# Moving the first eight dense products of a two-block decoder kernel into its key search

## The reference, cut to what matters

```python
q = (ht @ wq).reshape(t, 8, 2, 128)
sa, sb = scores of q[:, :, 0] and q[:, :, 1] against 128 keys each
va, ia = lax.top_k(sa, 16);  vb, ib = lax.top_k(sb, 16)
cand = va[..., :, None] + vb[..., None, :]          # 256 pairs for each of 8 heads
top, pos = lax.top_k(cand, 16)                      # 16 experts for each head
g = softmax(top)
a = gelu(einsum('thkd,td->thk', u_tab[eidx], ht))
out = einsum('thk,thkd->td', g * a, v_tab[eidx])
x = x + g2 * out
```

## Time and profile before

| | before |
|---|---|
| median of three runs (lowest, highest) | 2922.46 us (2916.36, 2926.57) |
| profiled execution, own time | 2922.81 us |
| its span | 2921.1 us |
| TensorE / VectorE / ScalarE / GpSimd busy, of the span | 87% / 52% / 29% / 26% |
| mean granted TensorE clock | 0.924 |
| bytes moved by DMA | 716.90 MB |

### The profile page before, as it was taken

The page is one execution under the profiler, slowest core; times in us unless marked ns, Lnnn a source line. Parts: engine busy times, 40 slices in busy tenths (PEclk is TensorE's granted clock), DMA queues, the critical chain, the costliest instruction groups (busy, mean ns, idle before and its releaser), DMA issues.

```text
span 2921.1 us, 35637 instructions
## 1 busy us (share of the span) xinstructions
PE 2540.6 (87%) x14451; PEld 1944.1 (67%) x14451; DVE 1505.6 (52%) x3249; ACT 837.0 (29%) x1443; POOL 773.5 (26%) x743
## 2 busy tenths in 40 slices
PE   5997998889688787779987947699999999999998
PEld 5684544457444444447764526699999998998887
DVE  3125565644200000025542899879988787864443
ACT  2114322133100000023431117634433343333332
POOL 0002310000100000010000019845565655524442
PEclk8997898999799899979988978899999999999999
DMA  8224400014599999962104002799999999979995
GB/s 324 106 90 177 170 29 29 29 61 173 233 421 423 420 423 421 422 259 87 58 29 158 1 0 84 235 385 393 342 378 377 375 373 349 381 297 367 367 362 210
DMA packets 191624, 716.90 MB, mean 245 GB/s; under 512 B 33176, under 2 KB 69056, under 8 KB 161888
## 3 DMA queue, kind: packets, MB, share of 16 engines
q1 hardware_dynamic: 128480, 488.06, 42.9%
q0 software_dynamic: 62976, 226.52, 20.4%
HBM read 658.02 MB, written 56.11 MB: 244 GB/s over the span
## 4 chain that ended last, share of the span: by engine, by line
PE 67%; DVE 13%; DMA 12%; ACT 3%; issue 2%; POOL 1%; SPq 0%; POOLq 0%; DVEq 0%; ACTq 0%
PE psum L3191 14%; PE psum L3178 12%; DMA arena<-w 8%; PE psum L1588 5%; PE psum L426 4%; PE psum L2608 4%; PE psum L2108 4%; PE psum L3140 3%; PE psum L929 3%; PE psum L1595 2%; PE psum L1201 2%; PE psum L1216 1%; PE psum L2259 1%; DMA arena<-v_rows,arena 1%; DVE arena L819 1%
## 5 line engine op out<-in xcount | busy, mean ns | idle before, releaser
L3191 PEld LDWEIGHTS psum<-rounded,rounded 128*128 128x128 f32 x3072 | 452.9, 188 | 28.1 <-issue 21.8
L3178 PEld LDWEIGHTS psum<-rounded,rounded 128*128 128x128 f32 x3072 | 453.5, 189 | 22.0 <-ACT rounded L3245 14.2
L3191 PE MATMUL psum<-rounded,rounded 128*128 128x320 f32 x3072 | 462.1, 311 | 5.9 <-DVE rounded L3262 5.9
L3178 PE MATMUL psum<-rounded,rounded 128*128 128x320 f32 x3072 | 461.8, 311 | 3.4 <-DVE rounded L3262 3.4
L3127 POOL DMA_INDIRECT arena<-u_rows,arena x192 | 282.2, 1470 | 255.0 <-DVE arena L3295 163.7
L3217 ACT ACTIVATE rounded<-arena 128x1024 fp32r<-128x1024 f32 x256 | 265.5, 1050 | 258.5 <-PE psum L3191 218.8
L1588 PE MATMUL psum<-arena 128*64 128x256 f32 x2048 | 262.4, 421 | 79.9 <-issue 60.6
L3262 DVE TENSOR_TENSOR rounded<-arena,rounded 128x1024 fp32r<-128x1024 f32 x256 | 312.1, 1220 | 25.2 <-ACT rounded L3217 25.2
L1588 PEld LDWEIGHTS psum<-arena 128*64 128x64 f32 x2048 | 183.4, 153 | 171.0 <-issue 124.3
L3127 POOL DMA_INDIRECT arena<-v_rows,arena x192 | 220.1, 1146 | 240.2 <-PE psum L3140 158.1
L1700 DVE COPY arena<-psum 128x256 f32<-128x256 f32 x32 | 13.6, 424 | 444.1 <-PE psum L1641 444.1
(11 more groups left out here) (441 smaller groups left out, 3341.4 us busy)
## 6 DMA issues: line engine op xcount, KB each, us to landing
arena<-w SPq DMA_DIRECT2D x96, 2048.0 KB, 27.4
arena<-uT SPq DMA_DIRECT2D x64, 1024.0 KB, 8.3
arena<-v SPq DMA_DIRECT2D x64, 1024.0 KB, 7.4
arena<-wada SPq DMA_DIRECT2D x12, 2048.0 KB, 8.8
arena<-wp SPq DMA_DIRECT2D x10, 2048.0 KB, 9.9
arena<-gd SPq DMA_DIRECT2D x64, 320.0 KB, 9.8
gd<-arena SPq DMA_DIRECT2D x8, 2048.0 KB, 17.1
xb<-arena SPq DMA_DIRECT2D x1, 12032.0 KB, 42.1
```

Of the source, the lines that this page charges most:

```text
L3178: ins = pe.matmul(PS[:, b, 0:DT], w[:, x, k, :], hv[:, y, :], k == 0 and i == 0, k == 7 and i == 2)
L3191: ins = pe.matmul(PS[:, b, 0:DT], w[:, y, x, :], gg[:, z, :], x == 0 and i == 0, x == 7 and i == 2)
```

## The change

It takes the eight u products of group 0 out of the dense stage and makes them between keys and gather. During the keys stage ScalarE copies the hidden rows and the raw weights of these eight units into rounded upper parts, and GpSimd subtracts to get the lower parts. SP loads the raw weights one unit (512 KB) at a time into space that the key weights have left. TensorE makes the eight products behind its last scores and ahead of `turn(0)`; ScalarE copies them out of PSUM (two before `exps(0)`, six after it) and SP writes them to a DRAM array `es`. Near the end of the gather stage SP reads them back (1.25 MB), and reads the first 256 columns of g for them (1 MB in four pieces); the last 64 columns are taken straight from tile 2 in SBUF. At the start of the dense stage ScalarE and VectorE do gelu, weighting and splitting of the eight before they go into their loops. The list `UNITS` is eight shorter (248), and the dots and rounds are spread again: few dots over 49 units, not 51, the other 128 over 121 units, not 125, the first 16 rounds every 7 units. On SP's queue, `g_piece(4)` and raw piece 3 now stand behind `write(2, 0)` and behind waits for VectorE's second weighted product and for that write's landing; X stays where it was, behind raw piece 5 and the last write.

```diff
+    Y = Stage(counter, "first products", "pe ac po")
+    FH = [alias(O_TEMP + 9216 + 4 * DT * i, 4 * DT) for i in range(4)]
+    o = O_TEMP + 9216 + 16 * DT
+    FU = [o, 0, 2048, 2 * RING, 2 * RING + 2048, 3 * RING, 3 * RING + 2048, RING]
+    assert o + 2048 <= 2 * O_TEMP
+    FUH = [alias(x, 1024) for x in FU]
+    FUL = [alias(x + 1024, 1024) for x in FU]
+    FP = [at(RING + 2048 + DT * i, DT) for i in range(6)] + [at(DT * i, DT) for i in range(2)]
...
+    FIRST_IN = ((0,), (1, 2), (3, 4), (5, 6), (7,))
+    FIRST_SPLIT = {4: 0, 6: 1, 7: 2, 10: 3, 11: 4, 13: 5, 14: 6}
...
+        for x, those in enumerate(FIRST_IN):
+            if x:
+                sp.wait_ge(*K.pe["q", x - 1, 3])
+            for u in those:
+                sp.dma_start(out=at(FU[u] + 1024, 1024), in_=A["uT"][u // 2, :, 1024 * (u % 2):1024 * (u % 2) + 1024]).then_inc(
+                    *d_fu[x]("unit", u))
         wait_all(sp, K)
         sp.wait_ge(*d_xs["hs"])
+        sp.wait_ge(*Y.ac["out", 5])
+        sp.dma_start(out=es[:, 0:6 * DT], in_=at(RING + 2048, 6 * DT)).then_inc(*d_es())
+        sp.wait_ge(*Y.ac["out", 7])
+        sp.dma_start(out=es[:, 6 * DT:8 * DT], in_=at(0, 2 * DT)).then_inc(*d_es())
...
+        for u in range(8):
+            pe.wait_ge(*Y.po["lower", u])
+            if u > 2:
+                pe.wait_ge(*Y.ac["out", u - 3])
+            else:
+                pe.wait_ge(*K.ac["q", 3, u])
+            w = [x[u][:, :].rearrange("p (k b) -> p k b", k=8) for x in (FUH, FUL)]
+            for k in range(8):
+                hv = first_rows(k // 2)[:, :, k % 2, :]
+                for i, (x, y) in enumerate(THREE):
+                    ins = pe.matmul(PS[:, u % 3, 0:DT], w[x][:, k, :], hv[:, y, :], k == 0 and i == 0, k == 7 and i == 2)
+            ins.then_inc(*Y.pe("product", u))
...
+        def first_split(u):
+            ac.wait_ge(*first_there(u))
+            ac.activation(FUH[u][:, :], at(FU[u] + 1024, 1024), ACT.Copy).then_inc(*Y.ac("upper", u))
...
+            ac.activation(first_rows(y)[:, 0], H2[:, 2 * y:2 * y + 2, 0:DT], ACT.Copy).then_inc(*Y.ac("rows", y))
...
+            if c in FIRST_SPLIT:
+                first_split(FIRST_SPLIT[c])
         scores(15)
+        first_split(7)
         wait_all(ac, K)
...
+            po.wait_ge(*Y.ac["rows", y])
+            v = first_rows(y)
+            po.tensor_tensor(v[:, 1], H2[:, 2 * y:2 * y + 2, 0:DT], v[:, 0].bitcast(F32), ALU.subtract).then_inc(*Y.po("rows", y))
+        for u in range(8):
+            po.wait_ge(*Y.ac["upper", u])
+            po.tensor_tensor(FUL[u][:, :], at(FU[u] + 1024, 1024), FUH[u][:, :].bitcast(F32), ALU.subtract).then_inc(
+                *Y.po("lower", u))
...
+        pe.wait_ge(*Y.ac["out", 7])
...
+            ac.wait_ge(*Y.pe["product", u])
+            ac.activation(FP[u], PS[:, u % 3, 0:DT], ACT.Copy).then_inc(*Y.ac("out", u))
+
+        product(0)
+        product(1)
         exps(0)
+        for u in range(2, 8):
+            product(u)
...
-    UNITS = [("u", 0, a) for a in range(8)]
+    UNITS = []
...
-        DOTS.setdefault(4 + 4 * k // 5 if k < FEW else 56 + 125 * (k - FEW) // 128, []).append(k)
-    WEIGHTS = {56: 0, 182: 1}
-    ROUND = {62 + 15 * r // 2: r for r in range(FEW_ROUNDS)}
-    ROUND.update({190 + 2 * r: FEW_ROUNDS + r for r in range(32)})
-    FOLD = {181: 0, 255: 1}
+        DOTS.setdefault(3 + 49 * k // 64 if k < FEW else 52 + 121 * (k - FEW) // 128, []).append(k)
+    WEIGHTS = {52: 0, 174: 1}
+    ROUND = {58 + 7 * r: r for r in range(FEW_ROUNDS)}
+    ROUND.update({182 + 2 * r: FEW_ROUNDS + r for r in range(32)})
+    FOLD = {173: 0, len(UNITS) - 1: 1}
...
+        sp.wait_ge(*d_gd[1][3]["g", 1])
+        sp.wait_ge(*d_es.end())
+        sp.dma_start(out=at(FB, 8 * DT), in_=es).then_inc(*d_first())
+        sp.wait_ge(*d_gd[1][0]["g", 1])
+        sp.wait_ge(*G.dv["h", 3])
+
+        for p in range(4):
+            sp.dma_start(out=at3(GSL[p], 2, DT)[:, :, 0:256], in_=gd[:, 2 * p:2 * p + 2, 0:256]).then_inc(*ring[3 + p]("g", p))
         wait_all(sp, G)
+        write(2, 0)
         sp.wait_ge(*d_small.end())
         sp.dma_start(out=H2S, in_=hs[:, :, DT:512]).then_inc(*d_hrest("rest"))
-        sp.dma_start(out=gd[:, 0:8, 256:DT], in_=g_of(2)[:, 0:8, :]).then_inc(*d_first())
-        write(2, 0)
...
+        sp.wait_ge(*E.dv["weighted", 0, 1])
+        sp.wait_ge(*d_gd[0][0]["g", 2])
+        g_piece(sp, 4)
         piece(3)
-        sp.wait_ge(*E.ac["split", 2])
-        sp.wait_ge(*d_first.end())
-        for p in range(4):
-            g_piece(sp, p)
         write(2, 1)
...
+        def product(a):
+            ac.activation(at(FB + DT * a, DT), at(FB + DT * a, DT), ACT.Gelu_apprx_tanh).then_inc(*E.ac("gelu", 0, a))
+
+        split(0)
+        split(1)
+        ac.wait_ge(*d_first.end())
+        product(0)
+        product(1)
+        split(2)
+        for a in range(8):
+            ac.wait_ge(*E.dv["weighted", 0, a])
+            if a == 3:
+                ac.wait_ge(*d_gd[0][0]["g", 2])
+            if a in (5, 6):
+                ac.wait_ge(*E.dv["gg", 0, 2 * a - 9])
+            ac.activation(gg_of(0, a)[:, 0, :], at(FB + DT * a, DT), ACT.Copy).then_inc(*E.ac("gg", 0, a))
+            if a < 6:
+                product(a + 2)
...
+        def product(a):
+
+            e, p = at(FB + DT * a, DT), a // 2
+            dv.wait_ge(*E.ac["gelu", 0, a])
+            dv.tensor_tensor(e[:, 256:DT], e[:, 256:DT], g_of(2)[:, a, :], ALU.mult).then_inc(*E.dv())
+            dv.wait_ge(*ring[3 + p]["g", p])
+            dv.tensor_tensor(e[:, 0:256], e[:, 0:256], at(GSL[p] + DT * (a % 2), 256), ALU.mult).then_inc(*E.dv("weighted", 0, a))
+
         wait_all(dv, G)
-        for j in range(AHEAD):
-            split(j)
-        dv.wait_ge(*d_hrest["rest"])
-        dv.tensor_copy(H2T.rearrange("p (k c t) -> p k c t", k=8, c=2),
-                       H2S[:, :, 0:FEW].unsqueeze(2).to_broadcast([128, 8, 2, FEW])).then_inc(*E.dv("twice"))
+        split(0)
+        split(1)
+        product(0)
+        product(1)
+        split(2)
+        for a in range(8):
+            gg = gg_of(0, a)
+            dv.wait_ge(*E.ac["gg", 0, a])
+            dv.tensor_tensor(gg[:, 1, :], at(FB + DT * a, DT), gg[:, 0, :].bitcast(F32), ALU.subtract).then_inc(*E.dv("gg", 0, a))
+            if a < 6:
+                product(a + 2)
+            if a == 3:
+                dv.wait_ge(*d_hrest["rest"])
+                dv.tensor_copy(H2T.rearrange("p (k c t) -> p k c t", k=8, c=2),
+                               H2S[:, :, 0:FEW].unsqueeze(2).to_broadcast([128, 8, 2, FEW])).then_inc(*E.dv("twice"))
```

More of the change, by code:

```diff
@@ L2560, in build, with first_rows, first_there @@
     WQ = (0, 2, 3, 1)
+    Y = Stage(counter, "first products", "pe ac po")
[6 more added lines that the diff above has]
+    FP = [at(RING + 2048 + DT * i, DT) for i in range(6)] + [at(DT * i, DT) for i in range(2)]
+    es = nc.dram_tensor("es", [128, 8 * DT], F32, kind="Internal").ap()
+    FIRST_IN = ((0,), (1, 2), (3, 4), (5, 6), (7,))
+    FIRST_SPLIT = {4: 0, 6: 1, 7: 2, 10: 3, 11: 4, 13: 5, 14: 6}
+    d_fu = [dma_counter(f"first{i}") for i in range(5)]
+    d_es = dma_counter("products")
+    def first_rows(y):
+        return FH[y][:, :].rearrange("p (s k t) -> p s k t", s=2, k=2)
+    def first_there(u):
+        x = (u + 1) // 2
+        return d_fu[x]["unit", FIRST_IN[x][-1]]
     def norm3_sums(pe, i):
@@ L2627, in keys_ac @@
             ac.activation(H2[:, k, :], H2[:, k, :], ACT.Identity, bias=MOD[:, 24 + k:25 + k]).then_inc(*N3.ac("shift", k))
+        ac.wait_ge(*N3.ac["shift", 7])
+        for y in range(4):
+            ac.activation(first_rows(y)[:, 0], H2[:, 2 * y:2 * y + 2, 0:DT], ACT.Copy).then_inc(*Y.ac("rows", y))
         for c in range(16):
@@ L2728, in build @@
     assert o <= O_IT
-    GGR = [alias(x, 2 * DT) for x in early + late]
+    FB = late[3]
+    assert late[6] == FB + 6 * DT
+    GGR = [alias(x, 2 * DT) for x in early + late[1:3] + late[3:5] + late[0:1] + late[5:7]]
     o = OW
@@ L2820, in one_hots, with product @@
                 *G.ac("hot", q4))
+        def product(u):
+            ac.wait_ge(*Y.pe["product", u])
+            ac.activation(FP[u], PS[:, u % 3, 0:DT], ACT.Copy).then_inc(*Y.ac("out", u))
+        product(0)
+        product(1)
         exps(0)
+        for u in range(2, 8):
+            product(u)
         for q4 in range(LEAD):
@@ L2829, in gather_ac @@
                     one_hots(q4 + LEAD)
+                if x4 == 0 and m == 1:
+                    ac.wait_ge(*d_es.end())
                 if x4 == 0 and m > 1:
@@ L3015, in build @@
     for k in range(ALL_DOTS):
-        DOTS.setdefault(4 + 4 * k // 5 if k < FEW else 56 + 125 * (k - FEW) // 128, []).append(k)
-    WEIGHTS = {56: 0, 182: 1}
-    ROUND = {62 + 15 * r // 2: r for r in range(FEW_ROUNDS)}
-    ROUND.update({190 + 2 * r: FEW_ROUNDS + r for r in range(32)})
-    FOLD = {181: 0, 255: 1}
```

(16 more changed lines are left out.)

2 lines of the change are left out of this document (removed).

## The result

In 20 timed runs of each, the kernel after took 2927.9 us as its median (2917.62 to 2935.54), the kernel before 2920.1 (2907.98 to 2928.82). The ratio is 1.0027, 95% interval 1.0015 to 1.004: slower by 7.8 us. The forecast was 2920, a little faster than before, in a range of 2902 to 2933. The time lies in that range, but the change is a small loss, not a small gain.

A forecast was written before the change was run, and what follows sets the result against it. It took TensorE and equally full DMA engines to bound the dense stage, and VectorE's search the keys stage's end. Terms -7.4 + 0.6 + 0 + 4.3 gave -2.5 on 2922.81: 2920.3, so 2920 us, range 2902 to 2933.

The forecast's parts named there:

- Removed, 28.16 us: Dense stage: eight u units of 24 matmuls go, 3.52 us each at the full clock, 28.16 us in all.
- the first reading: Dense stage: DMA engines as full as TensorE, so removed TensorE work frees time only where bytes come as much sooner.
- The products' new place, +0.6: Between keys and gather: three products at once, 9.6 us idle, five ending about 1.0 us after VectorE's pairs; cost +0.6 us.
- Rival C: Keys stage: GpSimd's subtractions hold up VectorE's search, up to 10 us beyond its slack, 2930 us; chance 0.05.
- The mutual exclusion: Keys search: GpSimd and two-input VectorE instructions shut each other out; seven pair sums, up to 17 us, within VectorE's slack.
- The start, -7.4: Start of dense stage: fourth v unit waits for X, landing about 1940.3, and ends at 1947.1, not 1954.55; 7.4 us gained.
- the forecast's own lower end: Start of dense stage: gathers take more of the DMA engines, X comes at 1946, and the gain is 1.7 us.
- Rival D: Start of dense stage: X lands at 1946 or later, TensorE isn't brought forward, 2926 us; chance 0.08.
- The rest of the dense stage, +4.3: First 16 rounds: all become short, so TensorE's waits for v rows go from 4.3 to 8.6 us, 4.3 more.
- rival B: Dense stage, 2050 to 2550: gathers become the bound, sixteen short rounds wait 1.5 to 2 us each, 2939 us; chance 0.13.
- B's turning point: First 16 rounds: from 0.7 us of waiting a round, the change turns slower than before.

The follow-up runs named there:

- products_only: Keys and gather stages of the kernel after, dense stage of the kernel before, so the eight products are made, stored, then made again: 2923.6 us, ratio 1.0001 to before.
- queue_order: Kernel after with X's transfer behind H2S, old densities, and raw piece 3 and the next write ahead of the waits and `g_piece(4)`: 2903.8 us; 2902.0 without that reordering.
- sched_only: Kernel before with nothing moved, only its dots and rounds spread as in the change: 2928.8 us, ratio 1.0031 to before.
- relaxed: Kernel after with the old densities back: 128 dots over 125 units, first rounds every 7 or 8 units; few dots stay denser: 2911.0 us, ratio 0.9971 to before.
- dots_only: Kernel after with only the 128 dots put back over 125 units, first rounds still every 7 units: 2917.7 us, ratio 0.9988 to before.
- x_early: Kernel after with X's transfer issued right behind H2S, ahead of `write(2, 0)` and raw pieces 3 to 5: 2912.6 us, ratio 0.9968 to before.

## Why the prediction was wrong

- **Removed, 28.16 us, and the first reading.** That the DMA engines were as full as TensorE, so that little of the 28 would come, held: 3.0 us of start was left of it.
- **The products' new place, +0.6.** Right, with its steps: 9.60 us of idleness where 9.6 was forecast, 19.45 us for five products against 20.2, -0.7 us in the table (with a spread of the starts above that size), and a ratio of 1.0001 for products_only. Rival C is out: 7.8 us of offset at every search step, VectorE busy 94.78 of 116 us against 93.48 of 115, with GpSimd 16.45 us beside it. The mutual exclusion that was weighed there was not put to the test: no pair sum stood beside a subtraction of GpSimd in the trace, only 121 instructions for maxima, indices and replacing, which took as long as before (an index search 0.264 us, a maximum 0.254 and 0.255).
- **The start, -7.4.** The mechanism was right (the fourth v unit waits 21.7 us for X, VectorE adds right behind the landing), the size was not: X lands 5.7 us later behind gather end, not 1.0 later. I had more bytes ahead of X moved at the rate of before, 354 GB/s. From just ahead of gather end (1889 and 1882) to X's landing 17.18 MB had taken 50.4 us (341 GB/s); now 18.02 took 56.3 (320 GB/s). The 0.84 MB more are gathered blocks (3.88 MB before, 4.72 after); SyncE's own queue moved 13.25 and 13.28. X was also issued 4.3 us later and not 5 sooner. SyncE's queue stood at the new waits ahead of `g_piece(4)` while the share fell to 0.84 and 183 GB/s (1890 to 1894), and 1918 to 1938 reads 1.02 where the earlier trace rows read 1.12; how much each of these costs isn't shown, and taking the first away (queue_order) brought nothing. On the clock of before X comes at 1945.1, close to the forecast's own lower end, 1946 with 1.7 us of gain. Rival D's number, 2926, comes near 2927.9, but D had 4.9 us for products and rounds where the table has 17.8: that is luck. Against products_only's 67.3 the gain is 5.5 us, against the profile of before 3.0.
- **The rest of the dense stage, +4.3.** The step that failed. I counted only the rounds' spacing, short rounds for long ones at the average wait of before. Measured: 11 us more of waits and 7 at the lower clock, which the term hadn't counted at all, 18.5 in all (15.7 against products_only). It is rival B's mechanism, the gathers as the bound; B's turning point was 0.7 us a round, and 15.3/16 is 0.96, if in five rounds and not in sixteen. sched_only shows it alone (+7.9 us), relaxed takes it away (-16.9). My term had four faults, with the clock. The dots' blocks use the same DMA and the same nine buffers, and were priced as VectorE work only; dots_only gives them about half of the loss. The ceiling was about right (409 GB/s at 1.02 while a round waits), but I compared it with a demand averaged over all units between two rounds, 386, and blocks came late with 364 delivered in the mean. And waits don't grow in step with the demand: the 12.4 us of landing were 17.36 in the chain.

What stays open: whether the same spread really costs more in the kernel after (17 us) than in the one before (8) and why, and what it would bring to gather the few dots' rows sooner. Half of x_early's 23 us goes to unit 54; the chain there names the landing of `gd`'s write, the u rows and VectorE, but no run took them out.

## What to carry to other kernels

When work is taken out of one place, its loop becomes shorter and everything spread over the loop becomes denser. Price that for each stream that shares a resource with the one that has to be on time, here every gathered block and not only those with a wait in the profile. Price it in the fullest stretch, not in the mean: beside a full TensorE and a mean DMA share of 0.97, a 3 to 7% denser plan cost more than the move brought. Here the spread was to be left alone (relaxed, 9.9 us under before) and the transfer that ends the first wait to be moved as well (x_early, 8.3): with both the same move brought 18.9 us.

## What the runs showed of the hardware

- A wait in a stream that is otherwise full cost more than its length: behind TensorE's waits of 7.1, 4.2 and 2.0 us the granted clock was at its lower level for 10.2, 6.8 and 3.4 us, and TensorE's work took 7 us longer. Behind a wait of 3.1 us in the kernel before it stayed at the upper one, and the round ran 1.92 us against 3.64.
- GpSimd's subtractions of 128x1024 beside VectorE's search for maxima and indices: no slower at all, while VectorE's multiplication with two inputs took 2.31 us beside GpSimd, against 1.22 for the reduction.
- An issue on SyncE's queue took 0.33 to 0.45 us for most transfers of the start, but 9.79 for a raw piece and 9.53 for X, in the timeline above, and 14.84 for a g piece in queue_order. What makes it long isn't shown.
- One gather buffer of nine was worth 17.4 us, at a mean DMA share of 0.92.
- A block of 512 KB landed 17.36 us behind its issue while the DMA engines moved 409 GB/s (share 1.02), against 12.4 and 9.6 in the rounds of before.
